# A fused decoder layer on one core: dealing the pieces and blocks of its dense pass over other picks

## What is computed

```python
idx = jnp.take_along_axis(cand_i, top_pos, axis=-1)
g = jax.nn.softmax(top_s, axis=-1)
u = peer_u[idx]
a = jax.nn.gelu(jnp.einsum('cd,chkd->chk', xc, u).astype(jnp.float32), approximate=False)
v = peer_v[idx]
return jnp.einsum('chk,chkd->cd', (g * a).astype(v.dtype), v).astype(xc.dtype)
```

## Time and profile before

| what | value |
|---|---|
| time, median of 3 runs | 3598.63 us (3596.17 to 3600.81) |
| time of the profiled execution | 3595.24 us |
| its span, first to last instruction | 3593.4 us |
| granted TensorE clock, mean | 0.917 |
| busy: TensorE, VectorE, GpSimd, ScalarE | 3075.4, 2611.0, 2267.4, 931.1 us |
| read from HBM, written | 1230.09 MB, 29.29 MB |

### The profile page before, as it was taken

How to read it: one execution, slowest core, us unless ns; L and a number is a source line. 1 busy time by engine, 2 the same in 40 slices (tenths; PEclk the granted TensorE clock), 3 DMA queues, 4 the chain that set the end, 5 groups by cost and what they waited for, 6 DMA issues and landing times.

```text
span 3593.4 us, 32998 instructions
## 1 busy us (share of the span) xinstructions
PE 3075.4 (86%) x9102; PEld 1566.1 (44%) x9102; DVE 2611.0 (73%) x6263; ACT 931.1 (26%) x2285; POOL 2267.4 (63%) x1942
## 2 busy tenths in 40 slices
PE   7897698799997898888997975459998898999988
PEld 4665344477554443333443421125543344544333
DVE  2218877897788988788898897978867768854555
ACT  2112242422123431153222221125410114520000
POOL 0006643687556667888876667776677676677775
PEclk9899797778999998999998998779999899999999
DMA  6359986899999999999999999998999999999999
GB/s 155 104 164 369 365 288 211 321 389 373 384 354 380 356 375 374 361 348 352 378 390 388 401 356 369 331 370 324 352 409 409 409 409 404 342 379 409 409 409 374
DMA packets 426300, 1261.64 MB, mean 351 GB/s; under 512 B 61063, under 2 KB 106791, under 8 KB 426106
## 3 DMA queue, kind: packets, MB, share of 16 engines
q0 software_dynamic: 276480, 1006.76, 73.3%
q1 hardware_dynamic: 141701, 247.01, 20.1%
q10 hardware_dynamic: 7936, 5.77, 0.5%
HBM read 1230.09 MB, written 29.29 MB: 350 GB/s over the span
## 4 chain that ended last, share of the span: by engine, by line
PE 38%; DMA 13%; POOL 12%; issue 10%; DVE 10%; SPq 3%; ACT 2%; another core or an unknown queue 1%; ACTq 0%; DVEq 0%; POOLq 0%
PE pY L1724 12%; DMA vbuf<-in_peer_v_dram,idx 7%; POOL ubuf L980 7%; PE pb L1697 6%; POOL vbuf L992 5%; PE pb L1346 4%; DVE ubuf L2408 4%; PE pb L1681 3%; PE pb L1610 2%; DMA ubuf<-in_peer_u_dram,idx 2%; PE pb L1638 2%; PE pb L1592 2%; PE pb L1449 1%; DVE acc L2429 1%
## 5 line engine op out<-in xcount | busy, mean ns | idle before, releaser
L980 POOL DMA_INDIRECT ubuf<-in_peer_u_dram,idx x1088 | 1298.4, 1193 | 871.0 <-issue 298.6
L2408 DVE CUSTOM_DVE_ANT_0 ubuf<-ubuf,hnf 128x1024 f32<-128x1024 f32 x967 | 1168.8, 1222 | 325.1 <-DMA ubuf<-in_peer_u_dram,idx 283.5
L1724 PE MATMUL pY<-vbuf,dg 128*128 128x512 f32 (+1 forms) x2076 | 1059.8, 641 | 222.1 <-DMA vbuf<-in_peer_v_dram,idx 117.1
L992 POOL DMA_INDIRECT vbuf<-in_peer_v_dram,idx x832 | 965.8, 1161 | 435.6 <-issue 217.2
L1724 PEld LDWEIGHTS pY<-vbuf,dg 128*128 128x128 f32 (+1 forms) x2076 | 381.0, 196 | 710.1 <-issue 517.7
L1697 PE MATMUL pb<-R 128*128 128x512 f32 x1024 | 463.6, 597 | 0.5 <-DMA R<-in_peer_v_dram 0.5
L2429 DVE SCALAR_TENSOR_TENSOR acc<-vbuf,gw,acc 128x1024 f32<-128x1024 f32 x313 | 402.1, 1285 | 64.8 <-DMA vbuf<-in_peer_v_dram,idx 57.0
L1592 PE MATMUL pb<-R 128*128 128x256 f32 (+2 forms) x1152 | 361.8, 475 | 10.4 <-DMA R<-in_w_in_dram 6.4
L1994 ACT ACTIVATE gel<-dots 128x4 f32<-128x4 f32 x272 | 55.4, 204 | 1106.4 <-DVE dots L2408 904.0
L1697 PEld LDWEIGHTS pb<-R 128*128 128x128 f32 x1024 | 196.4, 192 | 247.5 <-issue 245.9
L2004 ACT ACTIVATE dg<-ident,gw 128x128 f32<-128x128 f32 (+1 forms) x519 | 191.6, 385 | 380.0 <-DVE gw L2415 248.9
(11 more groups left out here) (260 smaller groups left out, 2730.4 us busy)
## 6 DMA issues: line engine op xcount, KB each, us to landing
R<-in_peer_v_dram SPq DMA_DIRECT2D x128, 512.0 KB
R<-in_w_in_dram SPq DMA_DIRECT2D x12, 2048.0 KB
R<-in_w_in_dram SPq DMA_DIRECT2D x24, 1024.0 KB
R<-in_w_query_dram SPq DMA_DIRECT2D x24, 1024.0 KB
ubuf<-in_peer_u_dram,idx POOLq DMA_INDIRECT x1088
vbuf<-in_peer_v_dram,idx POOLq DMA_INDIRECT x832
R<-in_w_out_dram SPq DMA_DIRECT2D x12, 1024.0 KB
R<-in_x_prompt_dram SPq DMA_DIRECT2D x16, 512.0 KB
```

Source lines behind the costliest of these rows:

```text
L980: pool.indirect_dma_start(out=ubuf[:, n % RING, :], out_offset=None, in_=peer_u[0], in_offset=bass.IndirectOffsetOnAxis(ap=idx[:, t % NI, ...
L992: pool.indirect_dma_start(out=vbuf[:, v % RING, :], out_offset=None, in_=peer_v[0], in_offset=bass.IndirectOffsetOnAxis(ap=idx[:, t % NI, ...
L1724: ins = pe.matmul(pY[0:rows, half, :], dg[:, CPE[m] % RDG, 0:rows], vbuf[:, v % RING, half * 512:(half + 1) * 512], start=first, stop=(t ! ...
L2408: dve.tensor_tensor_reduce(ubuf[:, n % RING, :], ubuf[:, n % RING, :], hn, 1.0, 0.0, ALU.mult, ALU.add, dots[:, q % 2, n % GRP:n % GRP + 1 ...
```

## The change

Two numbers of the table `cost` change: the entry of `dm` from 4.0 to 2.6, of `oh` from 1.2 to 3.0.

```diff
     def cost(stage, args):
 
         if stage in ("dm", "wm", "d_T"):
-            return {"dm": 4.0, "wm": 1.2, "d_T": 0.7}[stage], 0
+            return {"dm": 2.6, "wm": 1.2, "d_T": 0.7}[stage], 0
         if stage in ("oh", "dy", "d_ab"):
-            return 0, {"oh": 1.2, "dy": 1.3, "d_ab": 0.9}[stage]
+            return 0, {"oh": 3.0, "dy": 1.3, "d_ab": 0.9}[stage]
```

## The result

The changed kernel takes 3629.1 us (median of 4 runs, 3617.4 to 3634.1) where the kernel before, run beside it, takes 3597.4 (median of 4): a ratio of 1.0085 [1.0053, 1.0117], slower. The forecast was 3603 us; the time lies in the slower part of its range (3572 to 3640). Its +4 us are +32 between the medians and +22 between the profiled executions (3595.2 and 3617.4).

A forecast was written before the change was run, and what follows sets the result against it. Memory bounded the streams, the one-hot, scaling and product chain the weights stages; TensorE would bound the streams after. Stages 276 + 314 + 275 + 322 = 1187 against 1181, less 2 in the tail: +4 us, 3603 us, range 3572 to 3640.

The forecast's parts named there:

- What bounds the kernel, and the streams: Streams 1 and 2: bound passes from memory to TensorE, at 314 and 322 us, from 398 and 385.
- the 1% put on top: Stream 2: 1% added to TensorE's 318 us of work, giving 322 us.
- The slower rival: Streams: TensorE, as the bound, keeps losing what it lost as second engine; 22 us more, 3625 us; chance 0.22.
- The added picks: The 37 picks added to each weights stage: 107 us in the first, VectorE-bound; 108 in the second, POOL-bound.
- the 1.55: Weights 2, added picks: mean gather time if every dot were waited out in full; total +29 us, 3632; chance 0.03.
- The first 62 and 63 picks: Weights stages, first picks: fewer pieces per pick loosen the chain to 2.65 us a pick, 169 and 167 us.
- c = 1.47: Weights 1: price in us of a piece with its waits, from 3.27 us a pick being 1.75 + 1.03 c.
- weights stages over 290 us: Sign that the forecast is wrong: the chain in the weights stages did not loosen; 265 to 285 us were expected.
- Its sign for the streams, under 400 GB/s: Sign that the forecast is right: DMA under 400 GB/s in the streams, with TensorE over 97% busy.
- the faster rival: Weights stages run at the DMA floor, streams at TensorE's: 33 us less, 3565 us; chance 0.30.
- The tail: End of the kernel, 28 us: may lose 2 us, as the last v rows have landed when TensorE is late.
- A denser mix of blocks: Streams: denser blocks lower the DMA ceiling to 385 GB/s; +5 us, 3608 us; chance 0.02.

The follow-up runs named there:

- e7_own: The changed kernel with fewer v rows dealt to VectorE in the weights stages and more in the streams: 3523.2 us, 0.9991 of the kernel before.

## Why the prediction came out as it did

**What bounds the kernel, and the streams: right.** Memory bounded the streams before and TensorE bounds them after. They took 310.9 and 313.4 us for the forecast 314 and 322. The 318 us of TensorE's work in stream 2 were priced at 0.437 us a matmul, from a stream in which TensorE sometimes waited. Packed full it does 729 records in 312.7 us, 0.429 each, and the 1% put on top was not lost either. The slower rival, by which TensorE as the bound would keep its old waits, did not happen, though its 3625 us lie close to the measured 3629: in stream 2 its waits for v rows went from 19.4 us to none, as its groups show:

```profile
L1697 PE MATMUL pb<-R 128*128 128x512 f32 x512 | 228.2, 592 | 1.3 <-ACT R L1977 0.9 <-DMA R<-in_peer_v_dram 0.4
...
L1724 PE MATMUL pY<-vbuf,dg 128*128 128x512 f32 x219 | 102.3, 592 | 0.0
```

Nor did it wait for blocks beyond 7.8 us in six times over the span.

**The added picks: right.** In weights 2 the POOL pairs were to come every 2.92 us. Between the starts of the dots of picks 960 and 997 the changed kernel takes 110.9 us, 3.00 a pick, and on the chip without late releases 107.7, 2.91. There the row of POOL in the added picks reads:

```profile
L980 POOL DMA_INDIRECT ubuf<-in_peer_u_dram,idx x39 | 44.4, 1139 | 11.9 <-issue 11.0 <-DVE dots L2408 0.9
L992 POOL DMA_INDIRECT vbuf<-in_peer_v_dram,idx x39 | 42.9, 1100 | 11.9 <-issue 10.1 <-PE pY L1724 1.8
```

44.4 + 42.9 busy and 23.8 idle, nearly all of it "issue", fill the window's 110 us: POOL paces these picks. The mean of the two is 1.12 us. The Trainium skill's rule that the loser waits the other instruction out (SBUF — State Buffer, on who interferes with whom) was to give 1.55 were every pair to meet a dot; the measurement decides. But the mean mixes two kinds. Of the 77 gathers that start in this window (us 3065 to 3175) 43 took 0.94 us, most of them with a dot running beside them for a part of it, and the slowest took 1.93, 0.99 more, against a dot's 1.22. So a single meeting can cost nearly a whole dot, and what the 1.55 had too high is how many gathers meet one; this trace doesn't speak against the rule itself. The 37 picks added to weights 1 took 109.7 us (2.96) for the forecast 107, and 101.8 (2.75) on the better chip.

**The first 62 and 63 picks: the term that was mis-sized.** "I price a piece with its waits ... c = 1.47", with the waits shrinking along with the pieces per pick, gave 169 us for the first 62 picks. They took 187.0, 3.02 a pick (dot of pick 714 to dot of pick 776), outside its upper bound of 2.9. In weights 2 the time beside the 110.9 us above is 178 against the forecast 167. The four stages together missed by 25 us: 18 and 11 in these two terms, 6 in the added picks, less 12 in the streams, with 2 between the stages' edges. What the price assumed is that a stage's waits come from the chain itself. On the chip of the result a part of them does not: the "remote" waits on L1977 in the two weights stages went from 28 us (21.6 and 6.7) to 154 (86.8 and 67.0), their late part from 38 to 104, and the clock fell with them. By 2 x (1 - PEclk), TensorE spent some 65 and 63 us of the weights stages at 1.2 GHz, where it was 20 and 16. That a stage of 99 picks offers more occasions for them than one of 62 is an argument, not a run. The prediction's sign for this, weights stages over 290 us, came true in weights 1 (298.6), but what it named as the reason, a chain that did not loosen, did not: the one-hots' wait for the product fell from 18.7 to 5.4 us. Its sign for the streams, under 400 GB/s, was missed narrowly (401 and 405).

**And the same step on a chip without them** errs the other way: 161.3 us for the first 62 picks, 2.60 each, at the floor of 2.56 that the faster rival has. Weights 1 and 2, at 264.3 and 265.6 us, are the faster rival's 263 and 265. The total is not that rival's, since the kernel before is 72 us faster on such a chip as well and so has less left to win. So the +4 us of the forecast agree with one chip, where the difference is too small to tell from none, and not with the other two (+32 and +24 us between the medians), and both for reasons that the sum did not have: this agreement is luck in part.

**The tail: mis-sized.** "May lose 2 us" was the right mechanism; it lost 10 (30.6 to 20.4), the same in all profiles of the changed kernel.

**The side that was argued last.** A denser mix of blocks was to lower the ceiling, chance 0.02; stream 1 of `e7_own` has 64 blocks in 84 picks and moves 409 GB/s. The Trainium skill's 207 GB/s for rows pitched that far apart (DMA: Bandwidth & Descriptors, Latency and other measured facts) was read wrongly in the prediction: it is for copies between tensors in HBM with longer rows, and 214 is the full rate of such copies there, so it says nothing against packing the blocks.

**What stays open.** What a late release is. The profile names no releaser, and the runs show only where they occur (beside the result and on the second chip), on whom, and that they grow with the change. Most fall on an engine that waits for TensorE's product, most often at L1977, but not all. In the changed kernel VectorE once waits 7.74 us for a step of its own that is recorded as done at 2244.6:

```profile
2244.25 0.34 DVE L2342 TENSOR_TENSOR eq<-v 128x64 f32<-128x64 f32 x2
2252.32 0.28 DVE L2346 MAX8 top_s<-eq 128x8 f32<-128x112 f32 x1 [7.74 <-remote]
```

In the same six profiles 14 to 31% of the releases by TensorE, VectorE and ScalarE have no record, where the eight others lack next to none. So the recording itself differs between these chips; whether it holds the releases back, and whether the loss would be there without it, no run tells. That the late releases are the cause of the loss there, and don't merely go with it, rests on the chips compared and on the 24 us of idle time beside 8 of clock; in the changed kernel no run took them away by itself.

## What to carry to other kernels

Where two resources are nearly tied, spreading one stage's work over more slots can trade its bound for the neighbour's, as it did here: the sum saw 56 us of idle memory, and the best versions were 5 to 6 us under the kernel before, within the noise. Move the other movable work with it (the v rows, as in `e7_own`) and look at what the tail gives back. Price waits that the profile can't explain apart from those of the chain, and time a change of a few tenths of a per cent on more than one chip: the same two kernels differ by 0.85 and 0.87% on two chips and by 0.13% on a third.

## What the runs showed that I had not expected

- The kernel before takes 3526 us on two chips and 3584 and 3597 us elsewhere, and the difference goes with late releases: none in eight profiles of the two chips, 58 to 341 us of waits in the six others.
- A release by TensorE can reach ScalarE and VectorE 6 us after the recorded end of the product that it belongs to, at the same instant for both; and VectorE can wait 7.7 us for its own finished step.
- Extra products cost the old kernel 4 and 7 us in its weights stages where they gave TensorE 18 us more work in the first, and the late part of the waits at the 64 copies fell with them, from 31 to 6.5 us.
